# Expert rows added into the residual by accumulating transfers, and by one-hot products for the last two experts

## What is computed

```python
def hier_moe(h, gw, gb, ew, eb, w1, w3, w2):
    ...
    gate = jax.nn.softmax(top_v, axis=-1) * g_gate
    ...
    xs = xt[row_tok].reshape(n_blocks, MOE_BLOCK, d)
    def expert_block(args):
        xb, e = args
        return (jax.nn.silu(xb @ w1[e]) * (xb @ w3[e])) @ w2[e]
    ys = lax.map(expert_block, (xs, block_e)).reshape(n_rows, d)
    out = jnp.zeros((t, d), h.dtype).at[row_tok].add((ys * row_w[:, None]).astype(h.dtype))
```

## Time and profile before

| | us |
|---|---|
| median of 3 runs | 1759.94 (1758.48 to 1760.54) |
| the profiled execution | 1758.6 |
| its span in the profile | 1756.8 |
| TensorE busy | 1684.6 (96%) |
| VectorE busy | 1441.6 (82%) |
| ScalarE busy | 941.0 (54%) |
| GpSimd busy | 147.7 (8%) |
| mean granted clock of TensorE | 0.985 of full speed |

### The profile page before, as it was taken

The page is one execution under the profiler, slowest core; times in us unless marked ns, Lnnn a source line. Parts: engine busy times, 40 slices in busy tenths (PEclk is TensorE's granted clock), DMA queues, the critical chain, the costliest instruction groups (busy, mean ns, idle before and its releaser), DMA issues. The chain is left out here.

```text
span 1756.8 us, 24115 instructions
## 1 busy us (share of the span) xinstructions
PE 1684.6 (96%) x8776; PEld 1272.2 (72%) x8776; DVE 1441.6 (82%) x2045; ACT 941.0 (54%) x1218; POOL 147.7 (8%) x137
## 2 busy tenths in 40 slices
PE   7999999999999999999999999999999999999990
PEld 7768888877777777777777888867777777777760
DVE  6687958989789988678737986689898989898997
ACT  6533122133444455545565532277777777877762
POOL 1100000000000000000000000031212122211003
PEclk9999999999999999999999999999999999999995
DMA  5202132122354412412315941399999999999967
GB/s 210 72 1 85 54 105 93 60 84 73 122 185 127 146 55 67 144 55 83 110 37 202 337 171 66 126 381 392 402 390 404 395 402 393 403 391 402 403 275 287
DMA packets 77040, 359.82 MB, mean 205 GB/s; under 512 B 9020, under 2 KB 11612, under 8 KB 50588
## 3 DMA queue, kind: packets, MB, share of 16 engines
q1 hardware_dynamic: 67372, 325.14, 49.7%
q0 software_dynamic: 5888, 20.97, 3.6%
q10 hardware_dynamic: 3696, 12.59, 1.8%
HBM read 301.63 MB, written 55.99 MB: 204 GB/s over the span
## 5 line engine op out<-in xcount | busy, mean ns | idle before, releaser
L2768 DVE TENSOR_TENSOR wa_lo<-wa,w_hi 128x2048 fp32r<-128x2048 f32 x124 | 280.9, 2285 | 14.2 <-ACT w_hi L2652 13.1
L2652 ACT ACTIVATE w_hi<-wa 128x2048 fp32r<-128x2048 f32 x124 | 237.5, 1916 | 68.3 <-DMA wa<-expert_up 30.4
L1583 PE MATMUL psum<-h_hi,w_hi 128*128 128x512 f32 x512 | 210.3, 411 | 2.1 <-ACT gate_out L1245 1.6
L1583 PE MATMUL psum<-h_hi,w_lo 128*128 128x512 f32 x512 | 204.2, 399 | 0.0
L1583 PE MATMUL psum<-h_lo,w_hi 128*128 128x512 f32 x512 | 202.1, 395 | 0.0
L175 DVE MAX8 top<-sel 128x8 f32<-128x384 f32 (+5 forms) x192 | 171.3, 892 | 4.6
L173 DVE MATCH_REPLACE8 sel<-top,sel 128x384 f32<-128x384 f32 (+5 forms) x192 | 168.2, 876 | 0.0
L2776 DVE TENSOR_TENSOR wb_lo<-wd,w_hi 128x2048 fp32r<-128x2048 f32 x62 | 139.3, 2288 | 30.9 <-ACT w_hi L2662 30.9
L2548 PE MATMUL psum<-w_hi,xT_hi 128*96 128x512 f32 x508 | 162.0, 400 | 0.0
L2548 PE MATMUL psum<-wa_lo,xT_hi 128*96 128x512 f32 x512 | 159.7, 393 | 0.0
L2548 PE MATMUL psum<-w_hi,xT_lo 128*96 128x512 f32 x508 | 158.5, 393 | 0.0
(11 more groups left out here) (398 smaller groups left out, 3310.6 us busy)
## 6 DMA issues: line engine op xcount, KB each, us to landing
wa<-expert_up SPq DMA_DIRECT2D x128, 1024.0 KB, 22.0
wd<-expert_down SPq DMA_DIRECT2D x64, 1024.0 KB, 22.5
w<-w_gate SPq DMA_DIRECT2D x32, 512.0 KB, 4.1
gate_pre<-gate_out SPq DMA_DIRECT2D x64, 256.0 KB, 3.2
gate<-gate_pre SPq DMA_DIRECT2D x32, 512.0 KB, 6.0
ys<-yo ACTq DMA_DIRECT2D x31, 384.0 KB, 7.0
w<-w_T SPq DMA_DIRECT2D x18, 512.0 KB, 3.7
ys<-zeros SPq DMA_DIRECT2D x7, 1152.0 KB, 5.9
```

Of the source, the lines that this page charges most:

```text
L1583: ins = nc.tensor.matmul(psum[:, 7, :], w[:, k, :], x[:, k, half * 512:(half + 1) * 512], start=(n == 0), stop=(n == BURST - 1))
L2652: nc.scalar.activation(hi_a(i, j, q).rearrange("p c m n -> p (c m n)"), wa[j][q][:, :, :, :].rearrange("p c m n -> p (c m n)"), ACT.Copy). ...
L2768: nc.vector.tensor_tensor(wa_lo[j][q][:, :, :, :].rearrange("p c m n -> p (c m n)"), wa[j][q][:, :, :, :].rearrange("p c m n -> p (c m n)" ...
```

## The change

Four things, in words, then the diff.

1. Gates into results. `hot` is multiplied by the gates (VectorE, two operations behind `totals`), and sixteen small products on TensorE (`slot_gates`, behind the third up piece of expert 0) give `slot_gate`, the gate of each slot of each expert. `y_out` copies with that column as its scale, so `ys` holds gated rows.
2. Experts 0 to 29 by transfers. `early_rows` (five small operations on VectorE, at expert 30) makes `row_of` without the overflow blocks; a token whose expert is 30 or 31, or whose slot is over 96, gets a row of zeros. As soon as experts 28 and 29 are stored, GpSimd issues sixteen indirect transfers from `ys` straight into `x2[t]` with `compute_op=ALU.add`: first those of the first choice for all tiles, then those of the second, each of which waits until the first of its tile has landed.
3. Experts 30 and 31 by one-hot products. Their gated results aren't stored but kept as high and low parts in SBUF (`yl_hi`, `yl_lo`); `hotT[k]` (slots by tokens) comes from an iota and a comparison; `late` does 8 matmuls of 512 columns for each tile, 64 in all, into four pairs of PSUM banks in turn. VectorE's `late_adds` adds each pair of banks to `x2[t]`, when both transfers of the tile have landed.
4. The rest is moved. VectorE does all eight additions, then the overflow branch, and then in `combine` the eight reciprocals and scalings. The lists for the overflow and its additions go into the branch. `g_final` is loaded ahead of the branch.

```diff
+LATE = 2
+NO_ROW = (NE - LATE) * CAP
-        s.ys = dram("ys", [SLOTS, DM])
+        s.ys, s.ys_ov = dram("ys", [NO_ROW + 1, DM]), dram("ys_ov", [NO_ROW_OV + 1, DM])
...
         nc.vector.tensor_copy(s.totals[:, :], psum[:, 4, 0:NE]).then_inc(s.routed, 1)
+        for k in range(2):
+            ins = nc.vector.tensor_tensor(hot[:, k, :, :], hot[:, k, :, :],
+                                          s.gates[:, k, :].unsqueeze(2).to_broadcast([P, NT, NE]), ALU.mult)
+        ins.then_inc(s.gates_set, 1)
...
+        def slot_gates():
+            pe.wait_ge(s.gates_set, 1)
+            for k in range(2):
+                for t in range(NT):
+                    ins = nc.tensor.matmul(psum[0:CAP, 3, 0:NE], hot_c[:, k, t, :].bitcast(F32), hot[:, k, t, :],
+                                           start=(k == 0 and t == 0), stop=(k == 1 and t == NT - 1))
...
     def gpsimd(pool):
...
+        pool.wait_ge(a_used, 4 * (NE - 1))
+        pool.iota(tok_iota[:, 0:ZERO_ROW], pattern=[[1, ZERO_ROW]], base=0, channel_multiplier=0, **exact)
+        pool.iota(tok_iota[:, ZERO_ROW:], pattern=[[1, SEQ - ZERO_ROW]], base=ZERO_ROW + 1, channel_multiplier=0,
+                  **exact).then_inc(iota_set, 1)
+        pool.wait_ge(s.rows_set, 1)
+        for j in range(2):
+            pool.wait_ge(y_stored[j], 16 * (NE // 2 - 1))
+        for k in range(2):
+            for t in range(NT):
+                if k:
+                    pool.wait_ge(s.rows_in[t], 16)
+                col = k * NT + t
+                pool.indirect_dma_start(s.x2[t][:, :], None, s.ys,
+                                        bass.IndirectOffsetOnAxis(ap=s.row_of[:, col:col + 1].bitcast(U32), axis=0),
+                                        compute_op=ALU.add).then_inc(s.rows_in[t], 16)
...
     def tensor(pe):
...
+        def late(t, k):
+
+            for h in range(2):
+                if t == 0:
+                    pe.wait_ge(late_low, k + 1 + k * h)
+                for r, y in enumerate((yl_hi[k], yl_lo[k])):
+                    ins = nc.tensor.matmul(psum[:, late_banks(t) + h, :], hotT[k][:, t * P:(t + 1) * P],
+                                           y[:, h * 512:(h + 1) * 512], start=(k == 0 and r == 0),
+                                           stop=(k == LATE - 1 and r == 1))
+            if k == LATE - 1:
+                ins.then_inc(late_ready, 1)
...
     def scalar(act):
...
-            nc.scalar.activation(yo[j][:, :], y_banks().rearrange("p a b -> p (a b)"),
-                                 ACT.Copy).then_inc(y_taken, 1)
+            nc.scalar.activation(yo[j][:, :], y_banks().rearrange("p a b -> p (a b)"), ACT.Copy,
+                                 scale=s.slot_gate[:, bass.ds(i * 2 + j, 1)]).then_inc(y_taken, 1)
...
-        y_end(NE // 2 - 1)
+        y_late(1)
+        nc.scalar.activation(table[:, :], s.totals[:, 0:1], ACT.Sqrt)
...
     def vector(dve):
...
+        def late_adds():
+            for t in range(NT):
+                dve.wait_ge(s.rows_in[t], 32)
+                dve.wait_ge(late_ready, t + 1)
+                at = late_banks(t)
+                nc.vector.tensor_tensor(s.x2[t][:, :], psum[:, at:at + 2, :].rearrange("p a b -> p (a b)"),
+                                        s.x2[t][:, :], ALU.add).then_inc(s.summed, 1)
...
+        count_blocks()
+        late_rows()
+        late_lows()
+        late_adds()
...
 def combine(nc, a, s):
...
-        pool.wait_ge(s.rows_set, 1)
-        for t in range(NT):
-            for k, dst in enumerate((ya, yb)):
-                col = k * NT + t
-                pool.indirect_dma_start(dst[t][:, :], None, s.ys,
...
+        for t in range(NT):
             dve.wait_ge(rooted, t + 1)
             link(nc.vector.reciprocal(rms[:, t:t + 1], rms[:, t:t + 1]))
-            nc.vector.scalar_tensor_tensor(out=ya[t][:, :], in0=s.x2[t][:, :], scalar=rms[:, t:t + 1], in1=fg[:, :],
-                                           op0=ALU.mult, op1=ALU.mult).then_inc(final, 1)
...
+            nc.vector.scalar_tensor_tensor(out=out[t][:, :], in0=s.x2[t][:, :], scalar=rms[:, t:t + 1],
+                                           in1=fg[:, :], op0=ALU.mult, op1=ALU.mult).then_inc(final, 1)
```

More of the change, by code:

```diff
@@ L2459, in loop, with overflow @@
             body(NE // 2 - 1, j, False, j == 1)
-    def overflow(eng, body, before=None):
+    def overflow(eng, body, before=None, then=None):
         eng.wait_ge(ov_set, 1)
@@ L2526, in before, with then @@
             pool.sem_inc(ov["go"], 1)
+        def then():
+            pool.wait_ge(ov_listed, 1)
+            for n in range(2 * NT):
+                if n >= 2:
+                    pool.wait_ge(ov_added, n - 1)
+                col = n % 2 * NT + n // 2
+                pool.indirect_dma_start(ov_rows[n % 2][:, :], None, s.ys_ov,
+                                        bass.IndirectOffsetOnAxis(ap=s.ov_row[:, col:col + 1].bitcast(U32), axis=0)
+                                        ).then_inc(ov_in[n % 2], 16)
         def body(b):
@@ L2534, in body @@
             pool.sem_inc(ov["go"], 1)
-        overflow(pool, body, before)
-        for j in range(2):
-            pool.wait_ge(y_stored[j], 16 * (NE // 2 + j))
+        overflow(pool, body, before, then)
     def tensor(pe):
@@ L2613, in tensor @@
         down(NE // 2 - 1, 1, False, end=True)
+        def late(t, k):
[8 more added lines that the diff above has]
+                ins.then_inc(late_ready, 1)
+        pe.wait_ge(late_hot, LATE)
+        late(0, 0)
+        late(1, 0)
+        late(0, 1)
+        late(1, 1)
+        for t in range(2, NT):
+            if t >= 4:
+                pe.wait_ge(s.summed, t - 3)
+            for k in range(LATE):
+                late(t, k)
         def before():
@@ L2725, in body @@
             if last:
-                y_out(i, 0, False)
+                y_late(0)
                 return
@@ L2801, in blocks_of_experts, with late_rows @@
[L2801 to L2806, removed]
+        def late_rows():
+            link(nc.vector.tensor_copy(tok_f[:, :], s.tok_of[:, NE - LATE:NE]))
+            dve.wait_ge(iota_set, 1)
+            for k in range(LATE):
+                nc.vector.tensor_scalar(hotT[k][:, :], tok_iota[:, :], tok_f[:, k:k + 1], None, ALU.is_equal
+                                        ).then_inc(late_hot, 1)
@@ L2829, in body @@
             if last:
-                blocks_of_experts()
                 return
+            if end:
+                early_rows()
             for q in range(2):
@@ L2881, in body, with then @@
             glu(ov["half"], b + 1).then_inc(ov["hid"], 1)
-        overflow(dve, body, before)
+        def then():
+            for n in range(2 * NT):
+                t, k = n // 2, n % 2
+                dve.wait_ge(ov_in[k], 16 * (t + 1))
+                if k:
+                    dve.wait_ge(ov_added, n)
+                nc.vector.scalar_tensor_tensor(out=s.x2[t][:, :], in0=ov_rows[k][:, :],
+                                               scalar=s.gates[:, k, t:t + 1], in1=s.x2[t][:, :], op0=ALU.mult,
+                                               op1=ALU.add).then_inc(ov_added, 1)
+            dve.wait_ge(ov_added, 2 * NT)
+        overflow(dve, body, before, then)
     return Engines(sync=sync, gpsimd=gpsimd, tensor=tensor, scalar=scalar, vector=vector)
```

184 lines of the change are left out of this document (117 added, 67 removed).

## The result

| | before | changed |
|---|---|---|
| median of 16 runs each | 1758.36 us | 1763.38 us |
| ratio, 95% interval | | 1.0031 [1.0024, 1.0039] |
| span of the profiled execution | 1756.8 | 1760.6 |
| first transfer of results issued | 1712.80 | 1697.19 |
| last of the sixteen landed | | 1744.61 |

The changed kernel is slower by 0.3%, where I had forecast 0.3% faster (1755.1 us). The measured time is inside the range (1743.5 to 1768). The transfers did begin 15.6 us earlier than the gathers of before. All of that and more was given back.

What follows compares the result with a forecast made beforehand. TensorE bounds the experts, then a 47.6 us tail follows; last landing 1735.1 plus addition, overflow count, scalings and store gave 1752.0, 4.8 us less, so 1755.1 us for the median, range 1743.5 to 1768.

Steps and rivals of the forecast that it cites:

- the price of an adding transfer: At the sixteen transfers into the residual: 2.25 us for each 512 KB, 36.0 us in all.
- Rival 2: At the sixteen transfers: half rate exactly, 2.52 us each, 1759.4 us median, no change; chance 0.22 with prices 2.33 to 2.77.
- Rival 3: At the sixteen transfers: reads and write in turn, from 2.77 us each, 1767.1 us median at 3.0; chance 0.24.
- wait for the store of expert 29 ends, first issue: Ahead of the transfers: store issued at 1689.33, landed by 1697.0 beside the gain's load, first issue at 1697.3.
- first bytes behind the first issue: At the start of the transfers: bytes begin about 1.8 us behind the first issue, at 1699.1.
- sixteen transfers at the full rate: On the DMA engines: sixteen adding transfers take 36.0 us and the last lands at 1735.1.
- GpSimd's issues: On GpSimd: one transfer issued in 1.25 us, 20 us for sixteen, not the limit.
- Behind the last landing: At the end: last addition 1.3 us, overflow count 0.9, eight scalings 11.3, last store 3.4, ending at 1752.0.
- What cost nothing: Before the tail: gate products' 1.87 us fit TensorE's 2.37 us wait at expert 1; +0.25 us in all, bounds 0 and 0.5.
- The one-hot products: On TensorE behind the last down product: 64 matmuls 0.232 us apart, 14.85 us without pause, last banks ready at 1724.35.
- The place of the wait: Before VectorE's additions: DMA waits spaced some 2.25 us, up to about 1735.
- a sign of a wrong mechanism: At the one-hot products: TensorE at half clock would take 29.7 us and put the end at 1756.2.

Runs made afterwards that it cites:

- the last experiment: The changed kernel without the low parts of the down weights of experts 30 and 31, but for one column: 1760.53 us, ratio 1.0012 to the kernel before.
- with eight tiles: The changed kernel with first-choice rows copied for all eight tiles and each tile's finish among the additions: 1753.55 us, ratio 0.9972 to the kernel before.

## Why the prediction was wrong

**The failed step is the price of an adding transfer.** I took 2.25 us between 1.26 and 3.8, "since the two reads are from different memories I let a tenth of that overlap". There is no such saving: it takes 2.51 us, twice 1.26 to within the measurement. With plain copies the engines moved 415 GB/s again, so it is the adding and nothing else about these transfers. Why it takes twice the time, whether by the two reads or by something else in the transfer, no run here shows. Rival 2 had the price (2.52).

The Trainium skill, Collectives: The Full Stack, section The bandwidth ceiling: the fold count and why AG ≠ RS ≠ AR, states about half a copy's rate for the adding step of a reduce-scatter between ranks, and says that its model is for rings. The prediction carried that over to an indirect transfer within one core, and there the rate agrees, 209 for 415 GB/s.

Rival 3, a price of 2.77 us and more, is wrong. The sign came out as rival 3's all the same, because of the slow start and of the landing behind the last byte. That my range held the time (1763.38) is no merit of the sum: it was wide enough for prices up to 3.05 us.

**The rest of the sum**, term by term, to the last landing, 1735.1 forecast and 1744.6 measured:

| term | forecast | measured | off |
|---|---|---|---|
| wait for the store of expert 29 ends, first issue | 1697.3 | 1697.2 | -0.1 |
| first bytes behind the first issue | 1.8 | 3.8 | +2.0 |
| sixteen transfers at the full rate | 36.0 | 40.2 | +4.2 |
| slower rate at the start (120 GB/s to 1704, 185 to 1712) and at the end | 0 | 2.1 | +2.1 |
| end of the stream (about 1743.3) to landing | 0 | 1.3 | +1.3 |

The first issue was right by two errors that cancel: the store of expert 29 was issued 2.26 us late (1691.59), but landed in 4.76 us and not 6.9. VectorE's work on SBUF is 1.5 of the 2.0 us by which the first bytes were late, and 1.0 of the slow start: the last experiment gave these 2.5 us back. The landing behind the last byte I had put at nothing, though the earlier trace rows had a landing that is far longer than its 0.95 us of data. (A trickle of 20 GB/s runs on to 1744.0, so the border between the last two rows is mine.) GpSimd's issues I had at 20 us for sixteen; they took 33.3, to 1730.4, still 14 us ahead of the last landing.

**Behind the last landing** I had 16.9 us and there are 16.0: the overflow count costs VectorE 0.42 and not 0.9, the scalings are 1.39 apart and not 1.41, the last store takes 3.1. 9.5 - 0.9 = 8.6 us above the forecast span of 1752.0, which is the 1760.6. My sum with the half rate, 1756.3, would have been "no change"; the 4.3 us more make it "slower". So the price of a transfer took away the gain that I had forecast, and the terms that I had put too low or at nothing turned it into a loss.

**What cost nothing, and didn't.** The gate products were put at 1.87 us inside a wait of 2.37. That was a misreading of the earlier trace rows: its x16 counts records, two for each product, so the 1.87 us are for eight products (line 2245) and not for sixteen. The sixteen take 2.66. Most of the wait was gone too, since the up products ahead of them ended 1.9 us late; so the condition that I named ("if that wait were gone") came true. TensorE's loop ended 2.0 us later for a forecast of 0.25. The start of the transfers hangs on that loop too, by the store of expert 29; it cost little here only because the store's shorter landing made up for it. In a version that is bound by TensorE it would count.

**The one-hot products** were right for the first half: 0.227 us apart, ready without delay behind the down product (1711.23). With one choice only, all 64 ran so. The place of the wait was right too: DMA waits before all eight additions. In the middle the products paused for 9.09 us, which I had not foreseen, since four pairs of banks are too few when the additions wait for transfers; the twelve behind the pause ran at half clock, in part what I had named as a sign of a wrong mechanism. It cost nothing, since every addition waited for a transfer. And my reading that the clock of before was low only while TensorE did nothing holds for the earlier trace rows but not for that trace: at 1124 to 1128 it was 0.65 with TensorE busy throughout.

**Where the expected gain went.** The head start of 15.6 us and the two gated additions per tile that leave VectorE are real. But the doubled DMA time alone is 20 us for sixteen transfers, and the new order uncovers work on top: before, gathers, additions, scalings and stores ran side by side at 4.04 us a tile; now eight scalings stand behind the last landing. Covering the scalings alone gave 0.2%, since the stores then take their time from the adding transfers; copying the first choice alone gave 0.4%; both together gave 0.6%, so the two parts add up. Only both brought the kernel clearly below the one before.

## What to carry to other kernels

Before an addition is moved from an engine into a transfer, count the DMA engines' time with the adding transfers at twice their bytes, together with all stores that will run in the same stretch; the sum is a floor of the stage (50.2 us for 60.9 and 63.4 measured from issue to end, 40.2 for 53.6). Of two rows to be added, copy the first into a free buffer and add only the second in the transfer, which did better here than adding both, and let the finish of a tile run among the transfers. And look which engine works on SBUF while GpSimd issues its transfers: the first issues set when everything behind them begins.

## What the runs showed that I hadn't expected

- An adding transfer takes GpSimd 1.55 us to issue, a plain one of the same rows 0.94. It isn't the bound at 2.51 us a transfer.
- VectorE's subtractions from SBUF to SBUF (128x2048, 2.28 us each) hold up GpSimd's issue: 3.12 and 3.46 us instead of 1.60 and 1.54. Long issues beside the same subtractions show with plain copies too (third issue 3.48 for 0.94), and in the kernel before at expert 1's gather (2.84 for 0.93). Beside additions that read two tiles of SBUF the last two issues of the versions with copies took 1.9 to 2.2 us, but not every one was longer (with eight tiles, one at 1717.13 took 1.55 beside such an addition). Beside additions from PSUM they stayed at 1.55.
- A small float32 product of 32 columns counts as two matmuls, and sixteen take 2.66 us.
- Output stores and adding transfers share the engines by their work: each store of 512 KB puts off a landing by 1.3 us.
- From one profiled execution to the next TensorE's half-clock stretch near the router falls on other instructions, and the loop begins up to 6.7 us apart (expert 1's rows turned at 1151.79 with plain copies, at 1158.50 with the finish among the additions), though the program up to there is nearly the same. What starts it in one and not in another stays open.
